# Block two's beta, decay and branch gates computed in one unit with the two sparse values

## The chip, the cores and the metric

The kernel runs on one core of one Trainium2 chip. The metric is the device time of one execution in microseconds (us); the kernel before has a median of 890.23 us over 3 runs (889.27 to 891.12). TensorE (PE) multiplies, VectorE (DVE), ScalarE (ACT) and GpSimd (POOL) do the elementwise work, and SyncE (SP) issues the weight loads.

## The reference, cut to what matters

Two transformer blocks for 256 tokens of width 1024. The change is in the second block (names end in `_2`): its input is normed and multiplied by one wide matrix, whose columns are then split.

```python
h = rms_norm(x, mix_norm_gain)
proj = jnp.einsum('bsd,de->bse', h, w_in)
(qkv_a, z_a, beta_a, alpha_a, q_b, kc_b, vc_b, ks_b, vs_b, kw_b, vw_b,
 gate_b, merge_a, merge_b) = jnp.split(proj, split_at, axis=-1)
qkv_a = jax.nn.silu(causal_depthwise_conv(qkv_a, gdn_conv_w))
beta = jax.nn.sigmoid(beta_a.astype(f32))
log_decay = -jnp.exp(gdn_a_log) * jax.nn.softplus(alpha_a + gdn_dt_bias)
o_a = gated_delta_rule_chunked(q_a, k_a, v_a, beta, log_decay)
gates = jax.nn.sigmoid(gate_b.reshape(b_, s_, NSA_KV_GROUPS, NSA_GROUP_HEADS, 3))
o_b = native_sparse_attention(q_n, k_cmp, v_cmp, k_slc, vs_b, k_win, vw_b, gates, ...)
```

`beta_a` and `alpha_a` have 4 columns each, `gate_b` has 24, and the two values `vs_b` (selected) and `vw_b` (window) have 128 each.

## The kernel before, in words

**Projections.** The weights of a projection are cut into *units* of up to 2048 numbers per partition. Every unit passes through the same four steps. SP loads it into one of 5 ring slots as soon as the unit five places earlier in the list has been used. ACT rounds it to its high part (`highs`, line 1561), into one of 3 buffers, as soon as the unit three places earlier has been used. DVE subtracts that from the unit to get the low part (`lows`, line 2136). PE multiplies: each product is three matmuls, high by high, high by low and low by high (`three`, lines 519 to 521), and waits for `w_split`, the count of finished low parts. `project_channels` holds the weights stationary and moves 256 tokens past them, 48 matmuls for a unit of 256 columns. `project_tokens` holds tokens stationary and moves 256 weight columns, also 48 matmuls. `tokens_part` does the same for half of the inner dimension with 512 columns moving, 24 matmuls a half unit.

**Order.** Each engine runs its own written list. ACT and DVE put the splits between their other work by a rule: before they touch a result, `bank_ready` calls `highs` or `lows` up to the number of units that PE had taken when it finished that result, plus two. So a unit taken out of, or put into, PE's list moves the splits of the units behind it on ACT and DVE, and the loads behind it on SP.

**Around the change.** Block two's list of units reads: ma0 and ma1 (a merge gate, in four halves), beta, c0 to c5 (the 1536 convolved channels), kcks, kwvc, nq0, nq1, vsvw, w1k, w1v, z0, z1. In the small unit beta, 56 weight columns are stationary (4 beta, 4 alpha, 24 of padding, 24 branch gates). `high_parts_first` (lines 641 to 645) makes 24 matmuls, ACT copies the 56 rows to `gateT`, and after c0 PE turns them into tokens by two transposes (line 961, bank gtok). ACT takes the tanh, DVE's `gates` the sums, and between them they build `g_tok`, which the bank gc behind c2 needs.

DVE's convolution takes c0 to c5 in turn: low part of a later unit, 2 + 6 instructions (lines 2546 and 2548), silu (line 2535). Behind it come head products (line 998), the norms of the heads (PE line 1026, `ss`; POOL line 2075), the rope sums, the transposes kk and vt, and then the sh products (line 1045), which shift the compressed keys and values. DVE adds the block positions to sh in 16 instructions (line 2632). PE runs the unit vsvw between sh and the hidden layer `hid` (line 1056), which waits until DVE has read both sh banks. ACT copies vsvw to `v_tok`, read much later by `nsa_out`.

Of the kernel before, what the change touches and what calls it, by code (L numbers as in the profile page):

```python
# [22 lines left out]
S = 256  # L23
# [107 lines left out]
def build(nc, A, consts, out):  # L131
# [11 lines left out]
    with ctx:  # L143
# [105 lines left out]
        def tiled(off, a, b):  # L249
            return flat(off, a * b).rearrange("p (a b) -> p a b", a=a)  # L250
# [58 lines left out]
        raw, cv, ns = tiled(raw_at, 12, S + 3), tiled(cv_at, 12, S), tiled(ns_at, 8, S)  # L309
        v_tok, z2 = tiled(v_tok_at, TT, S), tiled(z2_at, 4, S)  # L310
        ma, mb = xn, tiled(mb_at, TT, D)
        gateT = prob[0:56, 0, 0:S]
        pcT = flat(xres_at, 8 * S, 16)
        egc = tiled(egc_at, 4, S)
        cols, gate_tok = tiled(cols_at, TT, 32), tiled(gate_at, TT, 24)
        tok = tiled(probT_at + 1024, TT, 56)
        alpha, soft, g_tok = (tiled(log_at + 8 * i, TT, 4) for i in range(3))
        kdt, kbe, vb = tiled(raw_at, 8, 128), tiled(raw_at + 1024, 8, 128), tiled(cv_at + 2048, 8, 128)
        nA, qkT = tiled(nA_at, 8, CH), tiled(qkT_at, 8, CH)
# [36 lines left out]
        def unit(name, *pieces, width=256):  # L356
            units[name] = (pieces, width)
# [30 lines left out]
            wide_units(f"bo{b}", A[w][0], 0, 2)  # L388
        wide_units("wo", A["w_o"][0], 0, 2)

        unit("beta", piece(w2, W2_OFF["beta"], 32, 0), piece(w2, W2_OFF["gate"], 24, 32), width=56)
        units_of("c", w2, W2_OFF["qkv"], 6)
        unit("kcks", piece(w2, W2_OFF["kc"], 128), piece(w2, W2_OFF["ks"], 128, 128))
        unit("kwvc", piece(w2, W2_OFF["kw"], 128), piece(w2, W2_OFF["vc"], 128, 128))
        unit("vsvw", piece(w2, W2_OFF["vs"], 128), piece(w2, W2_OFF["vw"], 128, 128))
        for j in range(2):
            unit(f"nq{j}", *(piece(w2, W2_OFF["q"] + 256 * g + 64 * (2 * j + r), 64, 128 * r + 64 * g)
                             for r in range(2) for g in range(2)))
# [72 lines left out]
        def _(pe):  # L471
# [121 lines left out]
                done(name, ins)  # L593
                unit_used[name] = full(name)

            def tokens_part(title, unit_name, x, k0, k1, last, tag=None, pair_ready=None, between=None):

                wh, wl = split_unit(unit_name, 512)
                for t in range(TT):
                    s = slice(128 * t, 128 * t + 128)  # L600
                    o = bank_of(f"{title}{t}")[:, :]
                    for k in range(k0, k1):
                        if tag is not None and t == 0:
                            pe.wait_ge(*read(f"T{tag}{k // 2}"))
                        if pair_ready is not None and t == 0 and k % 2 == 0:
                            pe.wait_ge(signal(pair_ready), k // 2 + 1)
                        ins = three(o, (x[0][:, k, s], x[1][:, k, s]), (wh[:, k - k0, :], wl[:, k - k0, :]),
                                    k == 0, k == last)
                    if k1 - 1 == last:
                        done(f"{title}{t}", ins)  # L610
                        unit_used[unit_name] = full(f"{title}{t}")
                    elif t == TT - 1:
                        part_done(unit_name, ins)
                    if between is not None and t == 0:
                        between()
# [12 lines left out]
            def wide_tokens(title, x, between=None, tag=None):  # L628
# [4 lines left out]
                if between is not None:  # L633
                    between()
                tokens_part(title, title + "b", x, 4, 8, KT - 1, tag)

            def high_parts_first(o, wh, wl, tag, low_ready):

                for i in range(KT):
                    pe.wait_ge(signal(f"high_{tag}"), i // 2 + 1)  # L640
                    mm(o, wh[:, i, :], h_hi[:, i, :], start=i == 0, stop=False, skip_group_check=True)
                    mm(o, wl[:, i, :], h_hi[:, i, :], start=False, stop=False, skip_group_check=True)
                for i in range(KT):
                    pe.wait_ge(*low_ready(i // 2))
                    ins = mm(o, wh[:, i, :], h_lo[:, i, :], start=False, stop=i == KT - 1, skip_group_check=True)
                return ins

            def identity_products(bank, n, tile=ident):

# [300 lines left out]

            first_gate()
            wide_tokens("ma1", (r_hi, r_lo))
            wh, wl = split_unit("beta", 56)
            bank = open_bank("ba")
            done("ba", high_parts_first(bank[0:56, 0:256], wh, wl, "y", lambda j: (signal("split_y"), j + 1)))
            unit_used["beta"] = full("ba")
            project_channels("c0", h_parts)
            pe.wait_ge(*read("ba"))
            bank = open_bank("gtok")
            for t in range(TT):  # L960
                ins = nc.tensor.transpose(bank[:, 56 * t:56 * t + 56], gateT[:, 128 * t:128 * t + 128], ident[0:56, 0:56])
            done("gtok", ins)
            project_channels("c1", h_parts)
            project_channels("c2", h_parts)
            pe.wait_ge(signal("consts2"), 16)
# [76 lines left out]
            for kv, tile in ((0, 0), (1, 3)):  # L1042
# [2 lines left out]
                    ins = mm(bank[:, 256 * g:256 * g + 256], const("selg")[:, 128 * g:128 * g + 128],  # L1045
                             ns[:, tile, :], start=True, stop=True)
                done(f"sh{kv}", ins)
            project_tokens("vsvw", h_parts)
            w = (plain_unit("w1k"), plain_unit("w1v"))
            bank = open_bank("hid")  # L1050
            for kv in range(2):
# [467 lines left out]
        def _(sc):  # L1519
# [297 lines left out]
            highs(splits_by["ma10"] + 2)  # L1817
            for t in range(TT):
                middle_gate("ma1", t)
            copy("ba", gateT, bank_of("ba")[0:56, 0:256])  # L1820

            def conv_tanh(j):
                tanh(f"conv{j}", pair(cv, j), wait=(signal("conv_done"), j + 1))

            for j in range(6):
                copy(f"c{j}", raw[:, 2 * j:2 * j + 2, 3:S + 3], bank_of(f"c{j}")[:, :].rearrange("p (a b) -> p a b", a=2))
                if j == 0:
                    bank_ready("gtok")
                    act(tok.rearrange("p a b -> p (a b)"), bank_of("gtok")[:, 0:112], ACT.Tanh, scale=0.5)\
                        .then_inc(signal("tok_tanh"), 1)  # L1830
                    sc.wait_ge(*read("gtok"))
                    step(act(soft, alpha, ACT.Abs))
                    step(act(soft, soft, ACT.Exp, scale=-1.0))
                    act(soft, soft, ACT.Ln, bias=1.0).then_inc(signal("alpha_ln"), 1)
                if j == 2:
                    bank_ready("gc")
                    gc = bank_of("gc")[:, 0:16].rearrange("p (t c) -> p t c", t=TT)
                    act(cols[:, :, 12:16], gc[:, :, 0:4], ACT.Copy)
                    act(cols[:, :, 4:8], gc[:, :, 0:4], ACT.Exp)
                    act(cols[:, :, 8:12], gc[:, :, 4:8], ACT.Exp).then_inc(bank_reader("gc"), 1)  # L1840
                if j >= 1:
                    conv_tanh(j - 1)
                if j == 3:
                    for b in range(2):
                        bank_ready(f"gb{b}")
                        act(pair(egc, b), bank_of(f"gb{b}")[:, :], ACT.Exp).then_inc(signal("egc"), 1)
# [14 lines left out]
            act(qkT, qkT, ACT.Exp).then_inc(signal("d_exp"), 1)  # L1861
            copy("nq0", pair(ns, 2))
            copy("nq1", pair(ns, 3))
            copy_tokens("vsvw", v_tok)

            def hidden_tanh():
                bank_ready("hs")
# [243 lines left out]
        def _(ve):  # L2111
# [380 lines left out]
            for j in range(4):  # L2492
                ve.wait_ge(signal("high_y"), j + 1)
                for k in (2 * j, 2 * j + 1):
                    ins = stt(h_lo[:, k, :], scaled_rows[:, k, :], gain["y"][:, k:k + 1], h_hi[:, k, :].bitcast(F),
                              ALU.mult, ALU.subtract)
                ins.then_inc(signal("split_y"), 1)
            def gates():

                bank_ready("gtok")  # L2500
                ve.wait_ge(signal("tok_tanh"), 1)
                tt_(alpha, bank_of("gtok")[:, 0:112].rearrange("p (t c) -> p t c", t=TT)[:, :, 4:8],
                    dt_bias.unsqueeze(1).broadcast_to([128, TT, 4]), ALU.add).then_inc(reader("gtok"), 1)
                tsc(cols[:, :, 0:4], tok[:, :, 0:4], 0.5, 0.5, ALU.mult, ALU.add)
                step(tsc(gate_tok, tok[:, :, 32:56], 0.5, 0.5, ALU.mult, ALU.add))
                ve.wait_ge(signal("alpha_ln"), 1)
                step(tsc(alpha, alpha, 0.0, None, ALU.max))
                step(tt_(alpha, alpha, soft, ALU.add))
                stt(g_tok, alpha, -1.0, a_pos.unsqueeze(1).broadcast_to([128, TT, 4]), ALU.mult, ALU.mult)\
                    .then_inc(signal("g_tok"), 1)  # L2510
# [25 lines left out]

            ve.wait_ge(signal("conv_pad"), 1)
            ve.wait_ge(signal("consts2"), 16)
            for j in range(6):
                lows(splits_by[f"c{j}"] + 2)  # L2540
                ve.wait_ge(*read(f"c{j}"))
                for tap in range(4):
                    for i in (2 * j, 2 * j + 1):
                        src, w = raw[:, i, tap:tap + S], conv_w[:, i, tap:tap + 1]
                        if tap == 0:
                            ins = tsc(cv[:, i, :], src, w, None, ALU.mult)
                        else:
                            ins = stt(cv[:, i, :], src, w, cv[:, i, :], ALU.mult, ALU.add)  # L2548
                    if tap < 3:
                        step(ins)  # L2550
                ins.then_inc(signal("conv_done"), 1)
                if j == 0:
                    gates()
                if j >= 1:
                    silu_of(j - 1)
                if j == 4:
                    decays()
# [376 lines left out]
```

## Time and profile before

| what | value |
|---|---|
| median of 3 runs | 890.23 us |
| span of the profiled execution | 888.7 us |
| median less that span (launch and end, outside the span) | 1.5 us |
| PE busy | 876.6 us, 99% of the span |
| DVE busy | 587.4 us, 66% |
| ACT busy | 441.7 us, 50% |
| DVE busy in 500 to 520, 540 to 560 and 560 to 580 us | 19.5, 19.5 and 17.6 of 20 us |
| PE idle in 520 to 540 and 540 to 560 us | 0.3 and 0.7 us |
| mean granted TensorE clock | 0.999 of full speed |

PE is busy nearly throughout, so whatever makes it do less or wait more moves the time. The share says nothing about how close the other engines are behind it: in three stretches DVE has almost no free time either. Matmuls overlap, so the pace of a row of matmuls is read from the distance of their starts and not from their durations.

### The profile page before, as it was taken

The numbers are of one execution on the slowest core, as the hardware profiler recorded it, in microseconds if no ns is written. First come the engines' busy times: TensorE is split into PE (matmuls) and PEld (weight loads), VectorE is DVE, ScalarE is ACT, GpSimd is POOL, SyncE is SP. The second block draws the span as 40 slices with busy tenths as digits, with TensorE's granted clock in tenths as the row PEclk, the third lists the DMA queues.
The fourth block names the chain that finished last, engine by engine and source line by source line (L and its number), as shares of the span: only waits on it lengthen the run. The fifth ranks groups of instructions, "written<-read, shape, count | busy, mean of one in ns | idle before, by whom it ended". The sixth has DMA issues, their size and how long they took to land.

```text
span 888.7 us, 13795 instructions
## 1 busy us (share of the span) xinstructions
PE 876.6 (99%) x5624; PEld 759.9 (86%) x5624; DVE 587.4 (66%) x898; ACT 441.7 (50%) x644; POOL 51.2 (6%) x78
## 2 busy tenths in 40 slices
PE   8999999999999999999999999999999999999997
PEld 6888999898999888888889999877788888888885
DVE  5775664565656756555686997956477777777544
ACT  6644444753345544544485652466254555555442
POOL 1000000000020110000020015200000100000000
PEclk9999999999999999999999999999999999999999
DMA  9757644456454554555747683412455556665541
GB/s 299 233 190 229 221 144 142 143 165 183 127 182 153 188 174 158 171 187 193 268 140 253 156 178 95 144 49 49 143 190 179 184 184 189 190 190 190 166 166 48
DMA packets 127813, 151.67 MB, mean 171 GB/s; under 512 B 16983, under 2 KB 93142, under 8 KB 127750
## 3 DMA queue, kind: packets, MB, share of 16 engines
q1 hardware_dynamic: 127466, 150.44, 54.4%
q8 instruction: 45, 0.74, 0.3%
q10 hardware_dynamic: 220, 0.28, 0.1%
q14 instruction: 18, 0.15, 0.0%
q0 software_dynamic: 64, 0.07, 0.0%
HBM read 148.67 MB, written 3.68 MB: 171 GB/s over the span
## 4 chain that ended last, share of the span: by engine, by line
PE 88%; DVE 8%; ACT 2%; issue 1%; DMA 1%; POOL 0%; POOLq 0%; SPq 0%; ACTq 0%; DVEq 0%
PE bank L519 18%; PE bank L521 18%; PE bank L520 18%; PE bank L1354 9%; PE bank L545 5%; PE bank L1355 5%; PE bank L546 3%; DVE w_lo L2136 2%; DVE arena L2548 1%; PE bank L1014 1%; PE bank L748 1%; PE bank L728 1%; PE bank L847 1%; DMA arena<-in_x 1%; PE bank L708 0%
## 5 line engine op out<-in xcount | busy, mean ns | idle before, releaser
L2136 DVE TENSOR_TENSOR w_lo<-ring,w_hi 128x2048 fp32r<-128x2048 f32 (+1 forms) x134 | 298.2, 2230 | 125.7 <-ACT w_hi L1561 125.3
L1561 ACT ACTIVATE w_hi<-ring 128x2048 fp32r<-128x2048 f32 (+1 forms) x134 | 248.9, 1860 | 98.4 <-PE bank L521 72.4
L519 PE MATMUL bank<-h_both,w_hi 128*128 128x256 f32 x488 | 140.3, 287 | 0.3 <-DVE w_lo L2136 0.3
L520 PE MATMUL bank<-h_both,w_hi 128*128 128x256 f32 x488 | 138.0, 283 | 0.0
L521 PE MATMUL bank<-h_both,w_lo 128*128 128x256 f32 x488 | 138.0, 283 | 0.0
L1354 PE MATMUL bank<-h_both,w_hi 128*128 128x512 f32 x352 | 124.8, 399 | 0.2 <-issue 0.2
L1355 PE MATMUL bank<-h_both,w_lo 128*128 128x256 f32 x352 | 98.8, 281 | 0.0
L519 PEld LDWEIGHTS bank<-h_both,w_hi 128*128 128x128 f32 x488 | 93.5, 192 | 2.3 <-issue 1.4
L520 PEld LDWEIGHTS bank<-h_both,w_hi 128*128 128x128 f32 x488 | 93.6, 192 | 0.1
L521 PEld LDWEIGHTS bank<-h_both,w_lo 128*128 128x128 f32 x488 | 93.5, 192 | 0.0
L1354 PEld LDWEIGHTS bank<-h_both,w_hi 128*128 128x128 f32 x352 | 66.1, 188 | 16.7 <-issue 0.4
L519 PE MATMUL bank<-w_hi,h_both 128*128 128x512 f32 (+1 forms) x192 | 73.7, 384 | 0.0
L521 PE MATMUL bank<-w_hi,h_both 128*128 128x512 f32 (+1 forms) x192 | 71.5, 372 | 0.0
L520 PE MATMUL bank<-w_lo,h_both 128*128 128x512 f32 (+1 forms) x192 | 71.4, 372 | 0.0
L1355 PEld LDWEIGHTS bank<-h_both,w_lo 128*128 128x128 f32 x352 | 66.5, 189 | 0.0
L1576 ACT ACTIVATE arena<-bank 128x512 f32<-128x512 f32 (+5 forms) x70 | 34.6, 524 | 61.8 <-PE bank L521 49.3
L545 PE MATMUL bank<-h_both,w_hi 128*128 128x512 f32 x128 | 45.3, 399 | 0.0
L1608 ACT ACTIVATE arena<-bank 128x512 f32<-128x512 f32 x24 | 14.2, 596 | 56.9 <-PE bank L521 56.9
L519 PEld LDWEIGHTS bank<-w_hi,h_both 128*128 128x128 f32 x192 | 36.2, 188 | 6.9 <-issue 0.7
L521 PEld LDWEIGHTS bank<-w_hi,h_both 128*128 128x128 f32 x192 | 36.2, 188 | 6.4
L520 PEld LDWEIGHTS bank<-w_lo,h_both 128*128 128x128 f32 x192 | 36.2, 189 | 5.9
L1743 ACT ACTIVATE arena<-arena 128x128 f32<-128x128 f32 (+1 forms) x48 | 21.3, 444 | 37.8 <-DVE arena L2379 37.8
(387 smaller groups left out, 1553.7 us busy)
## 6 DMA issues: line engine op xcount, KB each, us to landing
ring<-in_w_in SPq DMA_DIRECT2D x59, 1024.0 KB, 5.2
ring<-in_w_gate_up SPq DMA_DIRECT2D x44, 512.0 KB, 4.7
ring<-in_w_down SPq DMA_DIRECT2D x10, 1024.0 KB, 5.1
ring<-in_w_mem_kv SPq DMA_DIRECT2D x8, 1024.0 KB, 9.2
ring<-in_w_gla_out SPq DMA_DIRECT2D x4, 1024.0 KB, 5.0
ring<-in_w_x_out SPq DMA_DIRECT2D x4, 1024.0 KB, 5.2
ring<-in_w_dsa_out SPq DMA_DIRECT2D x4, 1024.0 KB, 5.7
ring<-in_w_o SPq DMA_DIRECT2D x4, 1024.0 KB, 5.0
```

The source lines that it names most:

```text
L519: mm(o, ah, bh, start=start, stop=False, skip_group_check=True)
L520: mm(o, ah, bl, start=False, stop=False, skip_group_check=True)
L521: return mm(o, al, bh, start=False, stop=stop, skip_group_check=True)
L545: mm(o[:, :], wh[:, i, s], both[:, :, i, :], start=i == 0, stop=False, skip_group_check=True)
L546: ins = mm(o[:, 0:256], wl[:, i, s], high[:, i, :], start=False, stop=i == KT - 1, skip_group_check=True)
L1354: mm(o[:, :], wh[:, k - k0, w], h_both[:, :, k, :], start=k == 0, stop=False, skip_group_check=True)
L1355: ins = mm(o[:, 0:256], wl[:, k - k0, w], h_hi[:, k, :], start=False, stop=k == KT - 1, skip_group_check=True)
L1561: act(w_hi[:, k % NHI, at:m], ring[:, order.index(name) % NSLOT, at:m], ACT.Copy)\
L1576: act(dst, src, ACT.Copy, scale=1.0 if scale is None else scale).then_inc(inc or bank_reader(name), 1)
L1608: act(tnh[:, i % 2, 0:n], src, ACT.Tanh, scale=0.5).then_inc(inc or signal("tanh_done"), 1)
L1743: ins = act(v, v, ACT.Exp, bias=neg_max[:, c:c + 1], scale=-1.0, accum_out=p_sum[:, c:c + 1])
L2136: tt_(w_lo[:, i, at:m], ring[:, i, at:m], w_hi[:, k % NHI, at:m].bitcast(F), ALU.subtract)\
```

## The change

The unit beta and the unit vsvw go. In beta's place come two half units, vga and vgb, each four of the eight slices of the inner dimension, with 288 columns: 128 of vs, 128 of vw, 24 branch gates, 4 beta and 4 alpha. Tokens are stationary and 288 columns move. The results of the 128 tokens of a tile lie in one bank, vg0 or vg1. The two transposes of gtok go, since the gates come out by tokens.

```diff
-        unit("beta", piece(w2, W2_OFF["beta"], 32, 0), piece(w2, W2_OFF["gate"], 24, 32), width=56)
+        for half in range(2):
+            k0 = 4 * half
+            unit(f"vg{'ab'[half]}", piece(w2, W2_OFF["vs"], 128, 0, k0, k0 + 4), piece(w2, W2_OFF["vw"], 152, 128, k0, k0 + 4),
+                 piece(w2, W2_OFF["beta"], 8, 280, k0, k0 + 4), width=288)
-        unit("vsvw", piece(w2, W2_OFF["vs"], 128), piece(w2, W2_OFF["vw"], 128, 128))
...
# PE
             wide_tokens("ma1", (r_hi, r_lo))
-            wh, wl = split_unit("beta", 56)
-            bank = open_bank("ba")
-            done("ba", high_parts_first(bank[0:56, 0:256], wh, wl, "y", lambda j: (signal("split_y"), j + 1)))
-            unit_used["beta"] = full("ba")
+            for t in range(TT):
+                open_bank(f"vg{t}")
+            for half in range(2):
+                tokens_part("vg", f"vg{'ab'[half]}", h_parts, 4 * half, 4 * half + 4, KT - 1, None, "split_y", None, 288)
             project_channels("c0", h_parts)
-            pe.wait_ge(*read("ba"))
-            bank = open_bank("gtok")
-            for t in range(TT):
-                ins = nc.tensor.transpose(bank[:, 56 * t:56 * t + 56], gateT[:, 128 * t:128 * t + 128], ident[0:56, 0:56])
-            done("gtok", ins)
...
-            project_tokens("vsvw", h_parts)
             w = (plain_unit("w1k"), plain_unit("w1v"))
...
# ACT
-            copy("ba", gateT, bank_of("ba")[0:56, 0:256])
+            for t in range(TT):
+                copy(f"vg{t}", v_tok[:, t, :], bank_of(f"vg{t}")[:, 0:256], inc=signal("v_tok"))
+                act(tok[:, t, :], bank_of(f"vg{t}")[:, 256:288], ACT.Tanh, scale=0.5).then_inc(signal("tok_tanh"), 1)
...
-            copy_tokens("vsvw", v_tok)
...
# DVE, called before the convolution of c0 and no longer behind it
+            def gate_sums():
+                for t in range(TT):
+                    bank_ready(f"vg{t}")
...
+                    tt_(alpha[:, t, :], bank_of(f"vg{t}")[:, 284:288], dt_bias, ALU.add).then_inc(reader(f"vg{t}"), 1)
+                tsc(cols[:, :, 0:4], tok[:, :, 24:28], 0.5, 0.5, ALU.mult, ALU.add)
+                tsc(gate_tok, tok[:, :, 0:24], 0.5, 0.5, ALU.mult, ALU.add)
```

The number of split units stays the same. One more of them stands ahead of c0 and one fewer behind nq1, so every split from c0 to nq1 keeps its place on DVE by the rule, and behind nq1 the splits of z0 and z1 come forward. The order of three pieces shows it. Line numbers of the two programs differ.

On DVE, ahead of the convolution: the rows begin with the low parts of the normed input, and `w_lo` of 448 is beta's. Before:

```order
L2495 SCALAR_TENSOR_TENSOR h_both<-arena,h_both 128x256 x8
L2136 TENSOR_TENSOR w_lo<-ring,w_hi 128x448
L2136 TENSOR_TENSOR w_lo<-ring,w_hi 128x2048 x3
L2546 TENSOR_SCALAR arena<-arena 128x256 x2
L2548 SCALAR_TENSOR_TENSOR arena<-arena 128x256 x6
L2502 TENSOR_TENSOR arena<-bank,arena 128x8
```

The same place now:

```order
L2477 SCALAR_TENSOR_TENSOR h_both<-arena,h_both 128x256 x8
L2118 TENSOR_TENSOR w_lo<-ring,w_hi 128x1152 x2
L2118 TENSOR_TENSOR w_lo<-ring,w_hi 128x2048 x2
L2486 TENSOR_TENSOR arena<-bank,arena 128x4 x2
L2487 TENSOR_SCALAR arena<-arena 128x2x4
L2488 TENSOR_SCALAR arena<-arena 128x48
L2118 TENSOR_TENSOR w_lo<-ring,w_hi 128x2048
L2534 TENSOR_SCALAR arena<-arena 128x256 x2
```

Two low parts of 1152 stand for one of 448, and the sums of the gates moved ahead of the first convolution.

On DVE, at the block positions (the row of 64x8x15 x16, line 2632 before and 2620 now), from the rope sums to the hidden layer's tanh. Before, the `w_lo` in these rows is z1's; z0's stands five rows above them:

```order
L2574 TENSOR_TENSOR arena<-bank,arena 128x512
L2620 TENSOR_TENSOR arena<-bank,arena 128x512 x2
L2574 TENSOR_TENSOR arena<-bank,arena 128x512
L2581 TENSOR_TENSOR arena<-arena 128x512
L2632 TENSOR_TENSOR arena<-bank,arena 64x8x15 x16
L2581 TENSOR_TENSOR arena<-arena 128x512
L2639 TENSOR_TENSOR arena<-arena 128x512
L2644 STREAM_TRANSPOSE arena<-arena 128x512
L2136 TENSOR_TENSOR w_lo<-ring,w_hi 128x2048
L2651 SCALAR_TENSOR_TENSOR arena<-arena,bank 128x2x30
```

Now, the five rows above are the same with z1's `w_lo` in z0's place, and it goes on:

```order
L2562 TENSOR_TENSOR arena<-bank,arena 128x512
L2608 TENSOR_TENSOR arena<-bank,arena 128x512 x2
L2562 TENSOR_TENSOR arena<-bank,arena 128x512
L2569 TENSOR_TENSOR arena<-arena 128x512
L2620 TENSOR_TENSOR arena<-bank,arena 64x8x15 x16
L2569 TENSOR_TENSOR arena<-arena 128x512
L2627 TENSOR_TENSOR arena<-arena 128x512
L2632 STREAM_TRANSPOSE arena<-arena 128x512
L2639 SCALAR_TENSOR_TENSOR arena<-arena,bank 128x2x30
```

One low part still stands ahead of the block positions; the one behind them is gone.

On PE, between the last products of sh (line 1045 before, 1030 now) and `hid` (line 1056 before, 1040 now). Before, the 48 matmuls of vsvw begin behind sh:

```order
L1007 MATMUL bank<-arena 128x128 x8
L990 MATMUL bank<-arena 128x512
L1045 MATMUL bank<-arena 128x256 x4
L519 MATMUL bank<-w_hi,h_both 128x256
L520 MATMUL bank<-w_lo,h_both 128x256
```

Now:

```order
L992 MATMUL bank<-arena 128x128 x8
L975 MATMUL bank<-arena 128x512
L1030 MATMUL bank<-arena 128x256 x4
L1040 MATMUL bank<-ring,arena 32x128 x32
L999 MATMUL bank<-arena 64x64 x16
```

`hid` directly follows sh.

## Rows read from the trace of the kernel before

**Rows 1.** PE's waits, whole run: who for whom, total us, times, longest.
```profile
PE bank L1126 <- ACT arena L1576: 1.5, 3, 0.6
PE bank L1056 <- DVE arena L2632: 0.5, 1, 0.5
PE bank L519 <- DVE w_lo L2136: 0.3, 1, 0.3
```

**Rows 2.** Chain that ended last, 514 to 560 us: start us, us, what.
```profile
518.09 2.21 DVE w_lo L2136
...
520.34 0.39 PE bank L519
...
537.26 2.94 POOL arena L2075
...
556.07 0.50 DVE arena L2632 x2
```

**Rows 3.** PE's timeline, beta and c0: start us, us, engine, line, operation.
```profile
473.62 0.28 PE L641 MATMUL bank<-h_both,w_hi 128*56 128x256 f32 x1
...
476.45 0.28 PE L519 MATMUL bank<-h_both,w_hi 128*128 128x256 f32 x1
...
482.29 0.33 PE L961 MATMUL bank<-arena 56*128 56x56 f32 x2
482.54 0.38 PE L519 MATMUL bank<-h_both,w_hi 128*128 128x256 f32 x1
...
483.00 0.28 PE L519 MATMUL bank<-h_both,w_hi 128*128 128x256 f32 x1
```

**Rows 4.** PE's timeline in ma1: two matmuls 33 places apart, 512 columns moving.
```profile
465.00 0.39 PE L520 MATMUL bank<-w_lo,r_hi 128*128 128x512 f32 x1
...
472.48 0.39 PE L520 MATMUL bank<-w_lo,r_hi 128*128 128x512 f32 x1
```

**Rows 5.** PE's timeline, sh, second and last matmul of vsvw, hid.
```profile
548.59 1.89 PE L1045 MATMUL bank<-arena 128*128 128x256 f32 x8
...
550.43 0.28 PE L520 MATMUL bank<-w_lo,h_both 128*128 128x256 f32 x1
...
555.94 0.28 PE L521 MATMUL bank<-w_hi,h_both 128*128 128x256 f32 x1
556.70 1.95 PE L1056 MATMUL bank<-ring,arena 128*32 128x128 f32 x64 [0.48 <-DVE arena L2632]
```

**Rows 6.** ACT's timeline, high parts of beta, of c1 and of z0.
```profile
466.95 0.58 ACT L1561 ACTIVATE w_hi<-ring 128x448 fp32r<-128x448 f32 x1
...
474.40 1.90 ACT L1561 ACTIVATE w_hi<-ring 128x2048 fp32r<-128x2048 f32 x1
...
538.90 1.92 ACT L1561 ACTIVATE w_hi<-ring 128x2048 fp32r<-128x2048 f32 x1 [4.88 <-DMA ring<-in_w_in]
```

**Rows 7.** DVE's timeline, low parts of beta, z0 and z1, block positions.
```profile
468.78 0.62 DVE L2136 TENSOR_TENSOR w_lo<-ring,w_hi 128x448 fp32r<-128x448 f32 x1
...
545.03 2.28 DVE L2136 TENSOR_TENSOR w_lo<-ring,w_hi 128x2048 fp32r<-128x2048 f32 x1
...
552.64 3.90 DVE L2632 TENSOR_TENSOR arena<-bank,arena 64x120 f32<-64x120 f32 x16
...
558.55 2.83 DVE L2136 TENSOR_TENSOR w_lo<-ring,w_hi 128x2048 fp32r<-128x2048 f32 x1
```

**Rows 8.** PE's timeline, its last matmul.
```profile
882.01 0.39 PE L521 MATMUL bank<-w_hi,f_lo 128*128 128x512 f32 x1
```

**Rows 9.** Windows after it: stretch, its us, busy us of each engine, PEclk, DMA, GB/s.
```profile
885.00:886.00 1.00, 0.00 (x0) 0.00 (x0) 0.49 (x1) 0.72 (x1) 0.01 (x1) 1.00 0.00 0
886.00:887.00 1.00, 0.00 (x0) 0.00 (x0) 0.00 (x0) 0.00 (x0) 0.00 (x0) 0.77 0.63 236
```

**Rows 10.** PE's timeline, 128x512 f32 products at the start and at 538 us.
```profile
1.04 5.24 PE L651 MATMUL bank<-arena 128*128 128x512 f32 x6 [1.04 <-DVE arena L2189]
...
537.98 1.56 PE L990 MATMUL bank<-arena 128*128 128x512 f32 x4
```

More of the change, by code:

```diff
@@ L311, in build @@
         ma, mb = xn, tiled(mb_at, TT, D)
-        gateT = prob[0:56, 0, 0:S]
         pcT = flat(xres_at, 8 * S, 16)
@@ L315, in build @@
         cols, gate_tok = tiled(cols_at, TT, 32), tiled(gate_at, TT, 24)
-        tok = tiled(probT_at + 1024, TT, 56)
+        tok = tiled(probT_at + 1024, TT, 32)
         alpha, soft, g_tok = (tiled(log_at + 8 * i, TT, 4) for i in range(3))
@@ L594, in project_tokens, with tokens_part @@
                 unit_used[name] = full(name)
-            def tokens_part(title, unit_name, x, k0, k1, last, tag=None, pair_ready=None, between=None):
-                wh, wl = split_unit(unit_name, 512)
+            def tokens_part(title, unit_name, x, k0, k1, last, tag=None, pair_ready=None, between=None, width=512):
+                wh, wl = split_unit(unit_name, width)
                 for t in range(TT):
                     s = slice(128 * t, 128 * t + 128)
-                    o = bank_of(f"{title}{t}")[:, :]
+                    o = bank_of(f"{title}{t}")[:, 0:width]
                     for k in range(k0, k1):
@@ L635, in wide_tokens @@
                 tokens_part(title, title + "b", x, 4, 8, KT - 1, tag)
[L637 to L646, printed above, removed]
             def identity_products(bank, n, tile=ident):
@@ L1827, in _ @@
                 if j == 0:
[L1828 to L1831, printed above, removed]
+                    sc.wait_ge(*read("vg1"))
                     step(act(soft, alpha, ACT.Abs))
@@ L2497, in _ @@
                 ins.then_inc(signal("split_y"), 1)
-            def gates():
[L2500 to L2505, printed above, removed]
+            def gate_sums():
+                for t in range(TT):
+                    bank_ready(f"vg{t}")
+                    ve.wait_ge(signal("v_tok"), t + 1)
+                    ve.wait_ge(signal("tok_tanh"), t + 1)
+                    tt_(alpha[:, t, :], bank_of(f"vg{t}")[:, 284:288], dt_bias, ALU.add).then_inc(reader(f"vg{t}"), 1)
+                tsc(cols[:, :, 0:4], tok[:, :, 24:28], 0.5, 0.5, ALU.mult, ALU.add)
+                tsc(gate_tok, tok[:, :, 0:24], 0.5, 0.5, ALU.mult, ALU.add)
+            def gates():
+                ve.wait_ge(*read("vg1"))
                 ve.wait_ge(signal("alpha_ln"), 1)
@@ L2538, in _ @@
             ve.wait_ge(signal("consts2"), 16)
+            gate_sums()
             for j in range(6):
```

## The prediction

> **What bounds the kernel now.** I read the shares first: PE is busy for 876.6 of 888.7 us, so the sum of PE's work is the first thing to price. Then I read PE's waits over the whole run [rows 1]. They come to a few us, and two of them stand inside the stretch that the change touches: 0.3 us at a projection that waited for its low part, and 0.5 us at `hid`, which waited for the block positions on DVE. Then the chain of waits between these places [rows 2], because two such short waits can mean that another engine is just behind. It is: the chain runs on DVE until 520.3 (kwvc's low part), on PE to 537, over POOL's norm (537.26), and on DVE without a break of note to the last block position at 556.57. From `hid` at 556.70 it is PE's again. So PE and DVE arrive at `hid` almost together: PE comes through vsvw 0.48 us early [rows 5]. The reader is to see that vsvw is not only work. It is what PE does while DVE gets ready.
>
> **Price of the new unit on PE.** With 256 columns moving, 46 steps of vsvw take 555.94 - 550.43 = 5.51 us, 0.1198 a step [rows 5]. With 512 columns, 33 steps take 7.48 us, 0.2267 a step [rows 4]. No row has 288. A line between the two gives 0.1198 + 32/256 x 0.1069 = 0.1332 us, and 48 matmuls 6.39 us. The bounds are the two paces themselves, 5.75 and 10.9 us; I take the line, since 288 lies next to 256, where the bottom bound is.
>
> **What goes.** Beta: from its first matmul at 473.62 to c0's at 476.45, 2.83 us [rows 3]. The transposes: c1 begins at 482.54, and its second group of three at 483.00 where 0.36 after an undisturbed start of 482.20 (476.45 + 48 x 0.12) would give 482.56, so gtok costs 0.44 us [rows 3]. Vsvw: sh ends at 550.48 and `hid` starts at 556.70 after 0.48 idle, 5.74 us [rows 5]. PE's work alone: 6.39 - 2.83 - 0.44 - 5.74 = -2.6 us.
>
> **When each piece falls.** At c1 PE is 6.39 - 2.83 - 0.44 = 3.1 us later than before. Is anything else late there? Priced by a line between 448 and 2048 numbers [rows 6, 7], a high part of 1152 takes 0.58 + 0.44 x 1.32 = 1.16 us and a low part 0.62 + 0.44 x 1.66 = 1.35 us; the two bounds are those rows. ACT can start vga at 466.95 and vgb at about 468.4, DVE ends them at about 471.5, and PE asks at 473.62: 2.1 us to spare. C0's high part now takes the place at 474.40 that was c1's, so its low part is there at 478.6 against PE's 480.0. C1's follows on vga's use at 476.8 and is there at 481.0 against 485.8. The copies of 128x256 and the small tanh on ACT and the sums on DVE fall in the gaps that both have up to c0. I cost them at nothing; without that cover they would be about 1.3 us of ACT and 0.5 of DVE.
>
> Through c0 to c5 DVE is the engine that sets the chain, and it gets no later start: its low part of c3 waits for ACT, which again comes through the decay's logarithm at about 488.3, as now. PE's 3.1 us of delay first use up DVE's slack. Conv by conv I find copies of c1 to c3 just in time and c4's about 1.4 us late. DVE's low part of kwvc is then done near 521.7, and PE asks for it at 523.4. So the wait of 0.3 us [rows 1] goes and PE stands at +2.8 us through kwvc and the norms. Low part z0 now stands ahead of the norms. Its slot is freed by kwvc at 529.2, 5.5 us of load as before the high part at 538.90 [rows 6] (freed at 533.4), then high and low part: done at about 539.1, against norms at 539.8. Hidden, with 0.7 us to spare.
>
> **What is late next.** POOL's norm and DVE's run of work begin only when PE has delivered the norms, so they move by the same 2.8 us. Between there and the last block position DVE's list has the same length as before: one low part of 2.28 us is still in it, z1's for z0's [rows 7]. Z1's load is freed by nq0 at 536.0, high part done near 543.5, asked for at 547.8: hidden. The last block position moves from 556.57 to 559.4 and `hid` from 556.70 to 559.5. PE reaches that wait at 550.48 + 2.8 = 553.3 and idles for 6.2 us instead of 0.48. The sum: -2.6 of work, +5.7 of idle, -0.3 of idle = +2.8 us. Equivalently: everything that vsvw's removal frees lies under DVE, and what stays is that the work ahead of DVE's run grew. Behind `hid`, DVE is freed of z1's low part (2.83 us [rows 7]), but PE hardly waits for it there; the largest wait is 1.5 us in three pieces behind ACT copies [rows 1] that hang on PE's own results. I count nothing back.
>
> **The clock.** PE never idles above about a us between its first and last projection, and the granted clock is 1.00 there. After its last matmul (882.01, over at 882.40) the clock is still 1.00 in 885 to 886 and means 0.77 in 886 to 887: it fell to 0.50, 1.2 GHz, at 886.5, 4.1 us after work ended [rows 8, 9]. An idle time of 6.2 us is longer than that, so I expect the fall inside it, and `hid` and what follows to start at half speed. The price: the six 128x512 products at the start pace at 0.87 us, four of the same kind at 538 us at 0.39 [rows 10]. The clock column shows 1.00 for both, so this rests on durations alone; six at the later pace would take 2.3 us, 2.9 less. Bounds for the loss here are 0 (the small products behind `hid` might not be bound by the array) and about 2.9. I take 2.5, near the row.
> The Trainium skill (TensorE: Matmul & The Clock Gate, Part 1) says that an idle PE drops to 1.2 GHz and must be busy for a while before it gets 2.4 GHz back, and that gaps in the middle of a kernel pay this again. The trace's end agrees with the first half; no run here shows the second. By that rule the time has the clock's 2.5 us in it; by the sum of PE's work alone it has not.
>
> **Forecast.** 888.7 + 2.8 + 2.5 = 894.0 us of span. The runs' median lies 1.5 us above the profiled span: 895.5 us. Own range of this case 893.6 to 897.5.
>
> **Rivals.**
> 1. The idle comes, the clock stays. For it: one fall in the trace, at the very end, after 4.1 us; a gap of 6.2 may just be seen differently. Then 888.7 + 2.8 + 1.5 = 893.0 us.
> 2. DVE gives the time back. DVE and ACT run up to 2.8 us ahead of PE behind `hid`, and all remaining waits, 1.5 + 0.5 [rows 1] with small ones, shrink, or PE's delay is taken up ahead of the norms by faster gates. Then +0.8: about 891.0 us. Against it: those waits are for ACT work on what PE has just made.
> 3. The other side, faster: DVE's run to the block positions is not tied to the norms as I read it. DVE no longer does vsvw's low part ahead of them, nor waits for gtok's logarithm; if that lets it reach the block positions early enough to meet PE, `hid` never waits, and PE's saving is all there: 888.7 - 2.6 - 0.8 + 1.5 = 886.8 us. It decides once DVE is 2.8 us earlier against PE than forecast; all is won at 6.2. Against it: POOL's norm at 537.26 starts when PE's norms end, and DVE's work behind it has no gap to shrink [rows 2].
> 4. 288 columns cost like 512, or the 32-byte pieces of the loads (8 columns) come late. At the upper bound the unit costs 4.5 us more: near 900 us.
>
> **Chances.** Forecast 0.62, rival 1 0.18, rival 2 0.07, rival 3 0.09, rival 4 0.04. A change of 0.2% (1.8 us) is about what a measurement of this kernel can tell from none; 892.0 is the border to slower. Rival 2 is mostly inside it. So faster 0.09, same 0.07, slower 0.84. The range is 891.8 to 897.8: it takes in the forecast, rival 1 and the clock's upper bound, and leaves out rivals 3 and 4.
>
> **What would show it.** In the new trace: 48 matmuls of 288 at 0.133 us; no wait for a low part of vga, c0 or kwvc; norms on PE about 2.8 us later than 533.4; one PE wait of about 6 us at `hid` on DVE's block positions, with PE's sum of waits up by 5.5; granted clock 0.5 in the few us behind it, with `hid`'s 64 records taking clearly more than 1.95 us; low part z1 ahead of the block positions. Wrong would be: the wait at `hid` under 3 us, or a PE step ahead of the norms that waits for DVE, or half speed that lasts much longer than 5 us.

## The result and the profile after

The changed kernel takes 895.85 us (895.07 to 896.06, 5 runs), the kernel before in the same comparison 891.10 us. The ratio is 1.0053, 95% interval 1.0041 to 1.0065: slower by 4.75 us. Measured once more beside e8, it took 895.16 against 890.88 us, 1.0052 (1.0037 to 1.0068). The profiled execution has a span of 893.8 us against 888.7.

PE's busy time is 876.5 us as before (876.6), though 26 matmul records are gone: at the half clock described below 96 others take 2.25 us more. PE's waits, whole run (who for whom, total us, times, longest), which answer to [rows 1]:

```profile
PE bank L1040 <- DVE arena L2620: 6.2, 1, 6.2
PE bank L1110 <- ACT arena L1560: 1.5, 3, 0.6
PE bank L666 <- DMA arena<-in_b_gla_a: 1.3, 1, 1.3
PE bank L641 <- DVE arena L2171: 1.0, 1, 1.0
PE bank L656 <- DVE arena L2146: 0.4, 1, 0.4
```

The wait at `hid` (line 1040 now) for DVE's block positions (line 2620) has grown from 0.5 to 6.2 us, and the wait for kwvc's low part is gone. The wait for the DMA of `b_gla_a` lies in the first microseconds of the program, far from the change; it was 0.7 us before. This execution reaches the place of the change 0.69 us later than the old one (474.31 against 473.62). The same kernel in e9 reaches it at 473.73, so this is not the change's doing and has to be taken off below.

The new unit on PE's timeline (start us, us, engine, line, operation), which answers to [rows 3]:

```profile
474.31 0.29 PE L520 MATMUL bank<-w_hi,h_both 128*128 128x288 f32 x1
...
480.56 0.29 PE L522 MATMUL bank<-w_hi,h_both 128*128 128x288 f32 x1
480.70 0.28 PE L520 MATMUL bank<-h_both,w_hi 128*128 128x256 f32 x1
```

48 matmuls in 480.70 - 474.31 = 6.39 us, 0.133 a step, without a gap at either half. C0 begins at 480.70 where it was 476.45.

The norms, sh and `hid` on PE, which answer to [rows 5], now:

```profile
536.46 3.74 PE L1011 MATMUL bank<-arena 128*128 128x128 f32 x32
...
551.83 1.89 PE L1030 MATMUL bank<-arena 128*128 128x256 f32 x8
559.90 3.64 PE L1040 MATMUL bank<-ring,arena 128*32 128x128 f32 x64 [6.19 <-DVE arena L2620]
563.47 1.71 PE L999 MATMUL bank<-arena 64*64 64x64 f32 x32
...
565.70 1.58 PE L1091 MATMUL bank<-arena 64*128 64x128 f32 x16
```

And the norms, level 1 and the logits before:

```profile
533.23 3.74 PE L1026 MATMUL bank<-arena 128*128 128x128 f32 x32
...
558.88 1.15 PE L1014 MATMUL bank<-arena 64*64 64x64 f32 x32 [0.23 <-DVE arena L2644]
...
560.54 1.58 PE L1107 MATMUL bank<-arena 64*128 64x128 f32 x16
```

`hid` follows sh after 6.2 us of nothing, and its 64 records take 3.64 us where they took 1.95. The 32 records of level 1 behind it take 1.71 for 1.15. The logits of line 1091 (1107 before, at 560.54) take their old 1.58.

DVE's and ACT's timelines of the same stretch answer to [rows 7] and [rows 6]:

```profile
512.99 0.62 DVE L2534 TENSOR_SCALAR arena<-arena 128x256 f32<-128x256 f32 x2 [1.37 <-ACT arena L1560]
...
536.68 2.29 DVE L2118 TENSOR_TENSOR w_lo<-ring,w_hi 128x2048 fp32r<-128x2048 f32 x1 [4.18 <-ACT w_hi L1545]
...
543.46 1.26 DVE L2585 TENSOR_TENSOR arena<-arena 128x8 f32<-128x8 f32 x1 [1.70 <-POOL arena L2057]
...
548.26 2.28 DVE L2118 TENSOR_TENSOR w_lo<-ring,w_hi 128x2048 fp32r<-128x2048 f32 x1
...
555.85 3.90 DVE L2620 TENSOR_TENSOR arena<-bank,arena 64x120 f32<-64x120 f32 x16
```

```profile
534.73 1.91 ACT L1545 ACTIVATE w_hi<-ring 128x2048 fp32r<-128x2048 f32 x1 [3.46 <-DMA ring<-in_w_in]
...
541.77 1.91 ACT L1545 ACTIVATE w_hi<-ring 128x2048 fp32r<-128x2048 f32 x1 [4.51 <-DMA ring<-in_w_in]
```

The first row is the fifth convolution step (c4), which now waits 1.4 us for ACT's copy of what PE has just made. Z0's low part is finished at 538.97, ahead of the norms' result at 540.2. Z1's (548.26) stands where z0's stood, and DVE works without a gap of note from 543.46 to the end of the block positions at 559.75.

PE's clock over the wait (stretch, its us, busy us of PE, PEld, DVE, ACT and POOL, granted clock, DMA, GB/s), which answers to [rows 9]:

```profile
553.00:556.00 3.00, 0.71 (x4) 0.29 (x2) 3.00 (x6) 0.00 (x0) 3.00 (x3) 1.00 0.00 1
556.00:558.00 2.00, 0.00 (x0) 0.00 (x0) 1.93 (x9) 0.00 (x0) 1.05 (x1) 0.98 0.00 0
558.00:560.00 2.00, 0.10 (x4) 0.13 (x8) 1.93 (x9) 0.00 (x0) 0.00 (x0) 0.50 0.00 0
560.00:562.00 2.00, 2.00 (x40) 2.00 (x43) 1.79 (x3) 0.00 (x0) 0.84 (x1) 0.50 0.00 0
562.00:564.00 2.00, 2.00 (x42) 1.62 (x35) 0.00 (x0) 0.28 (x1) 0.43 (x1) 0.50 0.00 0
564.00:566.00 2.00, 2.00 (x36) 1.87 (x34) 0.00 (x0) 0.96 (x3) 0.72 (x1) 0.81 0.62 150
```

The clock falls to 0.50 (1.2 GHz) just before 558, 4.2 us after sh ended, and comes back at about 564.8, after PE has been busy for 4.9 us.

**Where the 4.75 us come from.** At PE's steps, after minus before, less the 0.69 us of the start: c0 +3.6, norms +2.5, `hid` +2.5, the logits behind level 1 +4.5, and so to the end (span 5.1 - 0.7 = 4.4). So 2.5 us arise ahead of the norms and stay, and 2.0 us arise between `hid` and the logits, where the half clock costs 2.2 (1.69 at `hid`, 0.56 at level 1) and a wait of 0.2 at level 1 goes.

### The profile page after: what moved, and what is told of

Read it like the earlier page. It is cut to its first block, busy times and chain, and to the rows that moved or that the text cites. A ratio compares the mean times of both kernels' runs of the same rounds, so it can differ in the third digit from the quotient of the medians.

```text
span 893.8 us, 13748 instructions
## 1 busy us (share of the span) xinstructions
PE 876.5 (98%) x5598; PEld 760.8 (85%) x5598; DVE 587.0 (66%) x899; ACT 441.8 (49%) x645; POOL 50.1 (6%) x78
## 4 chain that ended last, share of the span: by engine, by line
PE 92%; DVE 4%; ACT 1%; issue 1%; DMA 0%; POOL 0%; POOLq 0%; ACTq 0%; DVEq 0%
PE bank L520 19%; PE bank L522 19%; PE bank L521 19%; PE bank L1338 9%; PE bank L546 5%; PE bank L1339 5%; PE bank L547 3%; PE bank L999 1%; PE bank L738 1%; DVE w_lo L2118 1%; PE bank L718 1%; PE bank L837 1%; PE bank L656 1%; PE bank L698 0%; DMA arena<-in_x 0%
## 5 line engine op out<-in xcount | busy, mean ns | idle before, releaser
L2118 DVE TENSOR_TENSOR w_lo<-ring,w_hi 128x2048 fp32r<-128x2048 f32 (+2 forms) x134 | 297.5, 2225 | 130.6 <-ACT w_hi L1545 130.2
L1545 ACT ACTIVATE w_hi<-ring 128x2048 fp32r<-128x2048 f32 (+2 forms) x134 | 248.8, 1859 | 98.2 <-PE bank L522 72.5
L520 PE MATMUL bank<-w_hi,h_both 128*128 128x512 f32 (+2 forms) x192 | 73.7, 384 | 0.0
L522 PE MATMUL bank<-w_hi,h_both 128*128 128x512 f32 (+2 forms) x192 | 71.7, 373 | 0.0
L521 PE MATMUL bank<-w_lo,h_both 128*128 128x512 f32 (+2 forms) x192 | 71.7, 373 | 0.0
L1560 ACT ACTIVATE arena<-bank 128x512 f32<-128x512 f32 (+4 forms) x70 | 34.4, 522 | 73.2 <-PE bank L522 47.9
```

Source lines behind the costliest of these rows:

```text
L520: mm(o, ah, bh, start=start, stop=False, skip_group_check=True)
L521: mm(o, ah, bl, start=False, stop=False, skip_group_check=True)
L522: return mm(o, al, bh, start=False, stop=stop, skip_group_check=True)
L1545: act(w_hi[:, k % NHI, at:m], ring[:, order.index(name) % NSLOT, at:m], ACT.Copy)\
L1560: act(dst, src, ACT.Copy, scale=1.0 if scale is None else scale).then_inc(inc or bank_reader(name), 1)
L2118: tt_(w_lo[:, i, at:m], ring[:, i, at:m], w_hi[:, k % NHI, at:m].bitcast(F), ALU.subtract)\
```

## The experiments

Each number is the median beside the kernel before on the same chip; ratios are to that kernel.

**e1: PE kept busy during the wait.** On the changed kernel:

```diff
             bank = open_bank("hid")
+            identity_products(bank, 6)
```

> The changed kernel with six 128x512 products of the identity on PE between sh and hid, written to hid's own bank before hid opens it, so nothing else moves. They take about 4.7 of the 6.2 us that PE waits there. Theory (the clock fell because PE idled, and this cost 2.2 us): the granted clock stays 1.00 from 550 to 570 us, hid's 64 records take 1.95 us again instead of 3.64, hid still starts when the block positions end, and the time is about 2.2 us below the changed kernel, 893.7. Rival (hid and what follows are slow for another reason, such as the queues being cold after the wait): hid stays above 3 us and the time stays at 895.9.

893.61 us, 1.0030 (1.0018 to 1.0041). PE's timeline, then the windows of the old slow stretch:

```profile
552.80 5.31 PE L641 MATMUL bank<-arena 128*128 128x512 f32 x12
559.15 1.95 PE L1041 MATMUL bank<-ring,arena 128*32 128x128 f32 x64 [1.04 <-DVE arena L2621]
```

```profile
558.00:560.00 2.00, 0.96 (x33) 0.88 (x36) 1.94 (x7) 0.00 (x0) 0.00 (x0) 1.00 0.00 0
560.00:562.00 2.00, 1.77 (x66) 1.53 (x57) 1.04 (x2) 0.28 (x1) 1.27 (x1) 1.00 0.00 0
```

The clock stays at 1.00, `hid` takes 1.95 us again and begins when it did (sh's start to `hid`'s start is 8.08 us, and 8.07 in the changed kernel). The time falls by 2.2 us against the changed kernel's first median, and by 1.55 against its second (895.16). From `hid`'s start to the logits' start it is 3.85 us here and 5.80 in the changed kernel's trace. That the lost clock costs time is shown; how much differs from execution to execution, as the last section says.

**e3: the two units early, but apart.** On the kernel before:

```diff
             unit_used["beta"] = full("ba")
+            project_tokens("vsvw", h_parts)
...
                 done(f"sh{kv}", ins)
-            project_tokens("vsvw", h_parts)
```

and `copy_tokens("vsvw", v_tok)` behind the copy of ba.

> The kernel before with vsvw moved behind beta and the two units still apart (beta 56 columns, vsvw 256, the transposes of gtok kept). It has the move alone, without the join. Theory: PE's sum of work is the old one; norms on PE 5.4 us later than before (5.74 less the 0.3 us wait), a wait of about 6.2 us at hid, clock falls there too; 890.9 + 5.4 + 2.2 = 898.3 us. The join alone is then worth -2.6 us (895.9 against 898.3). Rival (the loss comes from the 288-wide form or the joined gates, and not from the place): near 890.9.

898.15 us, 1.0079 (1.0066 to 1.0093). The norms begin at 539.07, 5.8 us later than before, and `hid` waits:

```profile
562.52 3.29 PE L1056 MATMUL bank<-ring,arena 128*32 128x128 f32 x64 [6.20 <-DVE arena L2632]
```

```profile
560.00:562.00 2.00, 0.00 (x0) 0.00 (x0) 1.93 (x9) 0.00 (x0) 0.00 (x0) 0.50 0.00 0
```

The loss is the move's: it costs 7.2 us here, and the join takes back 2.3 of them (898.15 less 895.85). So none of it has to be put down to the 288 columns or the joined gates. One detail was off: a low-part wait of 0.4 us remains at kwvc, which is why the norms are 5.8 and not 5.4 us late.

**e4: z1's low part behind the block positions.** On the changed kernel, on DVE:

```diff
+            ahead[0] = splits.index("z1")
             for t in range(TT):
                 bank_ready(f"kk{t}")
```

> The changed kernel with z1's low part (2.28 us on VectorE) moved back behind the block positions, where the kernel before had it. Theory (hid waits for VectorE's own list of work): block positions end and hid starts 2.3 us earlier, the wait falls from 6.2 to 3.9 us, which is shorter than the 4.2 us after which the clock fell, so it may also stay up: 893.6 us if it still falls, 891.4 if not. Rival (VectorE there waits for a transfer, POOL or PE, not for its own work): no change, 895.9.

893.69 us, 1.0030 (1.0018 to 1.0041).

```profile
548.38 0.69 DVE L2602 TENSOR_TENSOR arena<-bank,arena 128x512 f32<-128x512 f32 x1 [0.65 <-PE bank L992]
```

```profile
557.98 3.51 PE L1040 MATMUL bank<-ring,arena 128*32 128x128 f32 x64 [4.88 <-DVE arena L2621]
```

```profile
557.00:558.00 1.00, 0.02 (x3) 0.05 (x4) 0.95 (x5) 0.00 (x0) 0.00 (x0) 1.00 0.00 0
558.00:559.00 1.00, 1.00 (x24) 1.00 (x28) 1.00 (x2) 0.00 (x0) 0.00 (x0) 0.59 0.00 0
```

The wait falls to 4.9 us and not to 3.9: DVE now arrives early at kk and waits 0.65 us for PE there, so 1.3 of its 2.28 us are won. The clock stays at 1.00 through the whole wait and falls at about 558.2, when `hid` has been running for 0.2 us and 5.1 us after sh ended. It is back at about 561.6. From `hid` to the logits it is 5.17 us instead of 5.80, which gives another 0.6 of the 2.2 us. The direction holds (`hid` hangs on DVE's list), the size was 1 us too large.

**e2: other work in vsvw's old place.** On the changed kernel:

```diff
             w = (plain_unit("w1k"), plain_unit("w1v"))
+            z_half(0)
+            z_half(1)
             bank = open_bank("hid")
...
             nsa_step(1)
-            z_half(0)
...
-                    z_half(1)
```

with DVE's `z_copy(0)` and `z_copy(1)` ahead of the hidden sums.

> The changed kernel with other work in vsvw's old place: both halves of unit z0 (48 matmuls, 5.8 us) move from between the attention steps to between sh and hid, and VectorE's two copies of their results move ahead of the hidden sums. Theory (PE's saving of 2.6 us is real and was lost under the wait for VectorE): PE reaches hid within 0.5 us of the block positions, the clock stays up (-2.2 us) and the 5.8 us are gone from behind. Without new waits 887.9 us, 2.6 below the kernel before. Rival (the z0 halves were cover where they stood): PE waits for the softmax chain between the attention steps instead and most of the 5.8 us come back; then 889 to 893.7, at the top only the clock's 2.2 us are won.

889.80 us, 0.9987 (0.9978 to 0.9996): 6 us below the changed kernel and just below the one before. The time lies in the rival's range and above the theory's 887.9, but the reason is not the rival's: only about 2.0 of the 5.8 us come back, not most. PE's waits in the block:

```profile
PE bank L837 <- DVE arena L2377: 1.4, 2, 1.2
PE bank L1057 <- DVE arena L2620: 0.8, 1, 0.8
PE bank L1177 <- DVE arena L2678: 0.8, 1, 0.8
PE bank L999 <- DVE arena L2632: 0.2, 1, 0.2
```

The clock stays up, `hid` waits 0.8 us, and where the z0 halves had stood PE waits 1.2 us at attention step 2 and 0.8 at the compressed transposes.

**e6: ScalarE copies z0's results.** e2 with this in place of the two copies on DVE:

```diff
+            for n in range(2):
+                copy(f"z0{n}", z2[:, n, :], bank_of(f"z0{n}")[:, 0:256])
             copy("hid", hid_rows, bank_of("hid")[:, 0:128])
```

> e2 with only the two copies of z0's results moved from VectorE to ScalarE, z1's low part left where e2 has it. Theory: VectorE is 0.84 us earlier behind hid and not ahead of it, so the wait of 0.8 us at hid stays, and of the later waits (1.4 and 0.8 us) about 0.8 go: 889.0 us. Rival: as in e5, 889.8.

889.43 us (887.67 to 891.08), 0.9982 (0.9972 to 0.9993). The intervals of e2 and e6 overlap. In the trace `hid` waits 0.5 us, and the two later waits are the same 1.2 and 0.8 us, so the reason I gave is wrong: they do not depend on when DVE starts its list there.

**e5: and z1's low part much later.** e6 with z1's low part behind attention step 3, at 579.82 where e6 has it at 547.71:

```diff
+            ahead[0] = splits.index("z1")
             for t in range(TT):
                 bank_ready(f"kk{t}")
...
             rope_add(3, 6, 2)
-            ahead[0] = splits.index("z1") + 1
...
             nsa_step(3)
+            ahead[0] += 1
+            lows(ahead[0])
             nsa_step(4)
```

> e2 (both halves of z0 between sh and hid) with two things taken off VectorE's way: ScalarE, which has nothing to do there, copies the two results of z0, and z1's low part moves behind attention step 3, where VectorE waited 4.4 us. VectorE had 0.84 us of copies and, by e4, 1.3 us of low part ahead of what PE waited for. Theory (what is left of the 2.6 us hangs on VectorE's list): no wait at hid, the wait of 1.2 us for the attention norm behind level 2 shrinks to under 0.3, time 887.5 to 888.5 us. Rival (the z0 halves were needed as cover later on whatever VectorE does): the later waits stay, 889.0 to 889.8.

891.34 us (889.06 to 893.03), 1.0010 (1.0000 to 1.0020). Neither the theory (887.5 to 888.5) nor the rival (889.0 to 889.8) holds.

```profile
PE bank L520 <- DVE w_lo L2120: 2.0, 1, 2.0
PE bank L1112 <- ACT arena L1560: 1.5, 3, 0.6
PE bank L837 <- DVE arena L2379: 1.4, 2, 1.2
```

The wait at `hid` is gone as expected. But PE reaches unit z1 before DVE has its low part and waits 2.0 us, and again the 1.2 us at step 2 do not move.

**e7: the late low part alone, on the kernel before.** The same lines as in e5.

> The kernel before with z1's low part behind attention step 3 and nothing else. It asks how much of e5's gain has nothing to do with the join. Behind sh and vsvw PE waited 0.5 us at hid and 0.2 at level 1. Before, z0's low part stood ahead of the block positions and still does, so the theory says that hid's 0.5 us stays and at most 0.2 us goes: 890.6 to 891.0, no change. Rival (VectorE's relief is felt further on by itself): 890.0 or less.

889.37 us (888.53 to 891.34), 0.9988 (0.9979 to 0.9996). This is the rival's number, but the trace shows no reason for a gain: the waits at `hid` (0.5), kwvc (0.3) and level 1 (0.2) are those of the kernel before, whose own runs in this comparison spread from 888.92 to 891.63. Whether the 1.5 us are real stays open.

**e8: z1's low part where DVE waited.** e6 with e4's line, which puts the low part directly behind the block positions and the first turn.

> e6 with z1's low part directly behind the block positions and the first turn, ahead of the hidden sums, where e5's trace shows VectorE waiting 2.9 us for ScalarE. In e5 the low part stood 25 us later and PE waited 2.0 us for it at its next use. Theory: no wait at hid (as in e5) and no wait for a low part (as in e6); waits inside the block are the 1.2, 0.8, 1.5 and 0.2 us that e5 and e6 have both. Against e6 0.5 to 0.8 us less: 888.7 us. Rival (VectorE's low part there delays the first attention step and comes back as a longer wait at it): 889.4 or more.

889.02 us (888.56 to 889.38), 0.9979 (0.9970 to 0.9987). It beats both kernels, the changed one by 6.1 us in the same comparison. PE's timeline and DVE's:

```profile
559.38 1.95 PE L1057 MATMUL bank<-ring,arena 128*32 128x128 f32 x64
...
572.25 0.55 PE L837 MATMUL bank<-arena 128*128 128x128 f32 x3 [1.20 <-DVE arena L2379]
...
575.99 1.92 PE L1177 MATMUL bank<-arena 128*15 128x128 f32 x16 [0.77 <-DVE arena L2679]
```

```profile
560.43 2.84 DVE L2120 TENSOR_TENSOR w_lo<-ring,w_hi 128x2048 fp32r<-128x2048 f32 x1
...
563.88 0.29 DVE L2363 CUSTOM_DVE_ANT_0 arena<-bank,arena 128x128 f32<-128x128 f32 x1 [0.31 <-PE bank L1093]
```

`hid` no longer waits, and no low part is late. The 0.4 us against e6 lie inside e6's spread. Not shown is that the 1.9 us below the kernel before are owed to the join: the z0 halves were never moved in that kernel, and e7, which has no join and only a later low part, measured 1.5 us below it.

**e9: the changed kernel again.**

> The changed kernel as it is, once more, on the chip and in the rounds of e8: 895.9 us by the first measurement, 4.9 above the kernel before; the granted clock falls behind 553 us again and hid waits 6.2 us.

895.16 us, 1.0052 (1.0037 to 1.0068), with 6.2 us at `hid`. The clock falls here before 556:

```profile
553.00:556.00 3.00, 0.14 (x1) 0.00 (x0) 2.99 (x8) 0.00 (x0) 3.00 (x3) 0.97 0.00 0
556.00:558.00 2.00, 0.00 (x0) 0.00 (x0) 1.93 (x10) 0.00 (x0) 0.47 (x1) 0.50 0.00 0
```

## Why the prediction was right, step by step

- **The unit's price.** 6.39 us forecast, 6.39 measured: the line between the paces of 256 and 512 columns holds at 288.
- **Nothing late ahead of c0 and kwvc.** Right. The high parts of 1152 took 1.17 us and the low parts 1.31 each (1.16 and 1.35 forecast). The wait at kwvc went, and the fifth convolution step (c4) waited 1.4 us as worked out. Rival 4 is out.
- **Norms at +2.8 us.** +2.5 measured after the start is taken off, 0.3 too much in the sum. The term that was mis-sized is the wait at kwvc. PE is 3.1 us late up to the products behind c3 (line 980 before at 500.80, 965 now at 504.62), as forecast, and 2.5 us behind kwvc. The wait was priced at its listed 0.33 us, but the starts in the trace before show more:

```profile
519.74 0.28 PE L521 MATMUL bank<-h_both,w_lo 128*128 128x256 f32 x1
520.34 0.39 PE L519 MATMUL bank<-h_both,w_hi 128*128 128x256 f32 x1 [0.33 <-DVE w_lo L2136]
520.57 0.28 PE L520 MATMUL bank<-h_both,w_hi 128*128 128x256 f32 x1
```

Two steps that usually take 0.12 us each took 0.60 and 0.23, so 0.59 us went with the wait, nearly twice what the row lists as idle.

- **The wait at `hid`.** 6.2 us forecast and measured. E3 shows that it belongs to the place and not to the form, e4 and e2 that it is DVE's list against PE's cover.
- **The clock.** The fall inside the gap was right, also in e9 and e3. Its price was 2.5 us forecast; e1's median gives 2.2, and the steps from `hid` to the logits 2.0 in the changed kernel's trace and 1.3 in e9's, so the term was somewhat too large. The Trainium skill (TensorE: Matmul & The Clock Gate, Part 1) says that a gap within a kernel sends an idle PE back to 1.2 GHz and that it must earn 2.4 GHz again; at the time of the forecast only the first half had a row, and the windows after now show both. Rival 1, no fall, is out.
- **Nothing given back behind `hid`.** Right: the waits for ACT are 1.5 us in both traces, and DVE's freed 2.8 us became idle time of DVE. Rivals 2 and 3 are out.
- **The sum.** 5.3 us forecast, 4.75 measured (4.3 in e9); the two terms that were too large, 0.3 us at kwvc and 0.3 to 0.5 at the clock, make the difference. That the absolute time came within 0.4 us is partly luck, since the kernel before measured 0.9 us higher in the second comparison than in the runs that the forecast started from.

## What to carry to other kernels

Before a piece of work is removed from the bounding engine's list, look at the wait that follows it: if it ends on another engine that is busy without a gap, the piece was cover, and its removal turns work into idle time of the same length. If the saved work is also brought in ahead of what that other engine depends on, the whole chain moves back by it, and the idle engine may lose its clock on top. A saving of this kind has to come with a replacement for the cover; e8 made 6.1 us of difference by moving one projection and one low part and giving two copies to ScalarE.

## What the runs showed that I had not expected

- The fall of the clock came at different times after sh ended: 4.2 us in the changed kernel, 2.7 in e9, 2.2 in e3, and 5.1 in e4, where `hid` was already running. What it cost goes with how much of PE's work then fell under the half clock: 4.9 us of work in the changed kernel, about 3.3 in e9, 3.4 in e4 and 2.8 in e3. From `hid` to the logits these take 5.80, 5.14, 5.17 and 4.88 us, against 3.85 in e1 at full clock. So the same wait of 6.2 us cost 1.0 to 2.0 us through the clock, and one profile does not size it.
- The waits of 1.2 us at attention step 2 and of 0.8 us at the compressed transposes were the same to a few hundredths in e2, e5, e6 and e8, whatever DVE had ahead of them. In the changed kernel, where the z0 halves stand there, neither is listed; PE waits 0.2 us in all at that line. I take them to be the loop from PE's logits over DVE and ACT back to PE, which work on PE in between covers; no run takes that loop apart.
